# Reordering VectorE and ScalarE in the second mixer of a four-layer transformer kernel, with split gate-rank products and later splits

## What is computed

```python
def second_mixer(x):                                   # twice, L = 0 and 1
    h = rms_norm(x, norm_mix_g)
    p = h @ w_in                                       # 11 units of 256 columns, and 16 gate columns
    y_a = silu(layer_norm(conv31(a_val * sigmoid(a_gate))))     # 256 channels, 31 taps
    y_b = head_rms_norm(attention(q, k, v))                     # 4 heads
    gate_logit = p[..., 16 gate columns] @ gla_gate_w + gla_gate_b   # the gate rank
    log_a = log_sigmoid(gate_logit) / 16
    y_c = gla_chunked(q_c, k_c, v_c, log_a)            # memory: G = cumsum(log_a), state over 8 chunks
    y_c = head_rms_norm(y_c) * silu(p_r)
    return x + concatenate([y_a, y_b, y_c]) @ w_out    # 4 units
```

## Time and profile before

| | |
|---|---|
| time, median of 3 runs (lowest, highest) | 2444.72 us (2442.86, 2446.11) |
| the profiled execution's own time | 2447.14 us |
| its span, first to last instruction | 2445.2 us |
| PE busy | 2289.4 us (94%) |
| VectorE busy, ScalarE busy | 1758.5 us (72%), 1321.9 us (54%) |
| first mixer, L = 0 and 1: first product of T(0) | 19.4 and 435.7 us |
| second mixer, L = 0 and 1: transposes of the normed x | 1729.0 and 2087.8 us |
| end of the second mixer, L = 1: transposes for the feed-forward | 2237.4 us |

### The profile page before, as it was taken

One profiled execution on the slowest core, in us unless ns is written; L12 is line 12 of the kernel. 1 busy time (PEld: TensorE's weight loads), 2 busy tenths in 40 slices (PEclk: granted clock), 3 DMA queues, 4 the chain that ended last, 5 costly groups with the idle time before them and its releaser, 6 DMA issues.

```text
span 2445.2 us, 42024 instructions
## 1 busy us (share of the span) xinstructions
PE 2289.4 (94%) x16293; PEld 2136.1 (87%) x16293; DVE 1758.5 (72%) x1877; ACT 1321.9 (54%) x1254; POOL 185.5 (8%) x178
## 2 busy tenths in 40 slices
PE   7998998999699999999999999998788999798998
PEld 7898997899689999999999999998687998687997
DVE  4455555457478888888888888888676777666777
ACT  4543443554166767676767766766334444434443
POOL 1000000100000000000000000000580000660000
PEclk9999999999699999999999999999898999999999
DMA  9344655534379999999999999999323555323551
GB/s 299 104 139 142 203 187 175 153 105 145 98 272 343 347 336 352 332 353 345 341 349 335 350 333 351 334 350 332 111 88 111 173 198 176 119 95 104 191 176 63
DMA packets 423456, 556.71 MB, mean 228 GB/s; under 512 B 9746, under 2 KB 377092, under 8 KB 423344
## 3 DMA queue, kind: packets, MB, share of 16 engines
q1 hardware_dynamic: 419232, 544.85, 65.9%
q0 software_dynamic: 4112, 10.38, 1.4%
HBM read 554.13 MB, written 1.06 MB: 227 GB/s over the span
## 4 chain that ended last, share of the span: by engine, by line
issue 46%; PE 41%; DVE 5%; DVEq 3%; ACT 3%; DMA 1%; ACTq 0%; SPq 0%; POOL 0%; POOLq 0%
PE ps L616 12%; PE ps L617 12%; PE ps L618 12%; ACT w_hi L1305 2%; DVE w_lo L1691 1%; DVEq L2165 1%; PE ps L658 1%; PE ps L1187 1%; DVE cvT L2164 1%; PE ps L1132 1%; DVEq L1791 1%; PE ps L1167 1%; PE ps L807 0%; DMA raw<-in_w_in 0%; DVE x L1790 0%
## 5 line engine op out<-in xcount | busy, mean ns | idle before, releaser
L1691 DVE TENSOR_TENSOR w_lo<-raw,w_hi 128x2048 fp32r<-128x2048 f32 x519 | 1180.4, 2284 | 382.0 <-ACT w_hi L1305 380.4
L1305 ACT ACTIVATE w_hi<-raw 128x2048 fp32r<-128x2048 f32 x519 | 986.8, 1908 | 237.1 <-PE ps L618 223.3
L616 PE MATMUL ps<-w_hi,xg_hi 128*128 128x256 f32 x1792 | 515.6, 288 | 9.9 <-DVE xg_lo L2073 7.0
L616 PE MATMUL ps<-xT_hi,w_hi 128*128 128x256 f32 x1696 | 491.1, 290 | 17.4 <-DVE xT_lo L1706 8.4
L618 PE MATMUL ps<-w_hi,xg_lo 128*128 128x256 f32 x1792 | 504.6, 282 | 0.0
L617 PE MATMUL ps<-w_lo,xg_hi 128*128 128x256 f32 x1792 | 504.0, 281 | 0.0
L617 PE MATMUL ps<-xT_lo,w_hi 128*128 128x256 f32 x1696 | 485.8, 286 | 0.0
L618 PE MATMUL ps<-xT_hi,w_lo 128*128 128x256 f32 x1696 | 485.4, 286 | 0.0
L616 PEld LDWEIGHTS ps<-w_hi,xg_hi 128*128 128x128 f32 x1792 | 339.4, 189 | 17.4 <-issue 11.1
L616 PEld LDWEIGHTS ps<-xT_hi,w_hi 128*128 128x128 f32 x1696 | 331.9, 196 | 24.2 <-DVE xT_lo L1706 9.2
L617 PEld LDWEIGHTS ps<-w_lo,xg_hi 128*128 128x128 f32 x1792 | 339.5, 189 | 4.0
(11 more groups left out here) (444 smaller groups left out, 2809.9 us busy)
## 6 DMA issues: line engine op xcount, KB each, us to landing
raw<-in_exp_w SPq DMA_DIRECT2D x336, 1024.0 KB, 5.5
raw<-in_ffn_w_up SPq DMA_DIRECT2D x44, 1024.0 KB, 5.1
raw<-in_w_in SPq DMA_DIRECT2D x42, 1024.0 KB, 6.0
raw<-in_ffn_w SPq DMA_DIRECT2D x33, 1024.0 KB, 5.1
raw<-in_ffn_w_down SPq DMA_DIRECT2D x22, 1024.0 KB, 5.4
raw<-in_w_gate SPq DMA_DIRECT2D x16, 1024.0 KB, 5.4
raw<-in_w_out SPq DMA_DIRECT2D x8, 1024.0 KB, 4.9
raw<-in_w_o SPq DMA_DIRECT2D x6, 1024.0 KB, 5.6
```

The source lines that it names most:

```text
L616: pe.matmul(out, lhs[0], rhs[0], start=first, stop=False)
L1305: act.activation(w_hi[:, u.const % SPL, 0:width], raw[:, u.const % RAW, 0:width], ACT.Copy)\
L1691: dve.tensor_tensor(w_lo[:, u.const % SPL, 0:width], raw[:, u.const % RAW, 0:width], w_hi[:, u.const % SPL, 0:width].bitcast(F32), ALU.sub ...
```

## The change

Six things are altered, and nothing in what is computed but the rounding of the gate rank.

1. **Gate rank in split products.** VectorE splits `w16` into `w16_hi` and `w16_lo` once it has landed (`w16_split`), and PE's `gate_rank` makes 8 x 3 float32r matmuls for the float32 ones.
2. **The memory chain ahead of the taps.** VectorE's 13 taps, before in groups of 3, 2, 1, 3, 2 and 2 between the steps of the chain, come in groups of 4, 2, 3 and 4: four ahead of the gate logits, none from there until `atT` is masked. `ahead(3)` to `ahead(7)` each stand later in the chain, on VectorE and (`ahead(3)`) on ScalarE.
3. **PE:** head 0 of `gla_out` goes ahead of the attention scores, so PE waits for `state_ready` in front of both; the wait for `vb` moves from the first transposes to the first values.
4. **The end of the second mixer:** `gated(0)` ahead of `ahead(10)` on VectorE; the first `yM_lo` ahead of the attention's norm; on ScalarE `yM_hi` ahead of that norm's root, and `ahead(13)` ahead of the SiLU.
5. **Second splits behind the norm sums.** Of the two splits ahead of `sums_to_x` (and at the kernel's start, and at the experts' end) VectorE's second goes behind `x_parts`. ScalarE's halves stay.
6. **The z gate's sigmoid later.** `out(8)` and `out(9)` are plain copies, `out(8)` right after `am_ready`; one Sigmoid over all of `zg` follows the first pair of attention transposes (`zg_ready`).

Cut to its core:

```diff
@@ PE, gate_rank
-                    for i, part in enumerate((xT_hi, xT_lo)):
-                        for k in range(KC):
-                            m = pe.matmul(ps[0:16, 6, 0:S], w16[:, k, :], part[:, k, :].bitcast(F32),
-                                          start=i == 0 and k == 0, stop=i == 1 and k == KC - 1)
+                    pe.wait_ge(S_.w16_split, L + 1)
+                    pe.sem_inc(S_.pe_passed, 1)
+                    for k in range(KC):
+                        m = product(ps[0:16, 6, 0:S], [v[:, k, :] for v in (w16_hi, w16_lo)],
+                                    [v[:, k, :] for v in (xT_hi, xT_lo)], k == 0, k == KC - 1)
@@ PE, mixer2
                 pe.wait_ge(S_.state_ready, L + 1)
+                gla_out((0,))
                 pe.wait_ge(S_.proj2_out, L * 11 + 8)
                 scores(0, (2, 3))
                 scores(1, (4, 7))
-                gla_out()
+                gla_out((1, 2, 3))
                 tok(8)
...
-                pe.wait_ge(S_.proj2_out, L * 11 + 9)
                 pe.wait_ge(S_.expd2, L + 1)
                 next_pair(0)
-                tok(9, lambda: next_pair(1))
+
+                def first_values():
+                    pe.wait_ge(S_.proj2_out, L * 11 + 9)
+                    next_pair(1)
+
+                tok(9, first_values)
@@ ScalarE, mixer1
                 act.activation(stat[:, 24:32], ps[:, 2, 8:16], ACT.Exp, scale=-1.0).then_inc(S_.am_ready, 1)
+                out(8, zg[:, :, 0:256], bank(0, TT, 256))
                 act.drain()
...
                 split(u + 11)
-                out(8, zg[:, :, 0:256], bank(0, TT, 256), ACT.Sigmoid)
                 split(u + 12)
-                out(9, zg[:, :, 256:512], bank(1, TT, 256), ACT.Sigmoid)
+                out(9, zg[:, :, 256:512], bank(1, TT, 256))
+                act.drain()
...
                 pT_pair(0)
+                act.activation(zg[:], zg[:], ACT.Sigmoid).then_inc(S_.zg_ready, 1)
                 pT_pair(1)
@@ ScalarE, mixer2
                 act.activation(egT[:], egT[:], ACT.Ln, bias=1.0).then_inc(S_.gln_ready, 1)
+                ahead(3)
...
-                square_root(S_.sqrt2_in, S_.sqrt2_out, L * 5 + 3, stat[:, 112:120])
                 act.wait_ge(S_.yc_psum, L * 2 + 1)
                 high(yM_hi[:, 0:2, :], 3, 70)
+                square_root(S_.sqrt2_in, S_.sqrt2_out, L * 5 + 3, stat[:, 112:120])
...
+                ahead(13)
                 act.wait_ge(S_.cnorm_ready, L + 1)
...
-                ahead(13)
                 ahead(14)
@@ VectorE, mixer1 and mixer2
                 x_parts(L * 12, 4)
+                split(u + 1)
                 split(u + 2)
...
+                split(u + 1)
                 ahead(0)
                 ahead(1)
+                dve.wait_ge(S_.p2_loaded, L * 192 + 192)
+                dve.tensor_copy(w16_hi[:], w16[:])
+                dve.drain()
+                dve.tensor_tensor(w16_lo[:], w16[:], w16_hi[:].bitcast(F32), ALU.subtract).then_inc(S_.w16_split, 1)
...
                 ahead(13)
-                ahead(14)
                 sums_to_x(u + 14, L * 6 + 3, None, half_square, OUT2_BANKS)
...
                 x_parts(L * 8 + 28, 0)
+                ahead(14)
@@ VectorE, main
-                    split_next(Count(LAYER1_UNITS))
+                    split(Count(LAYER1_UNITS))
                     sums_to_x(Count(LAYER1_UNITS - 1), 0, ALPHA, half_stats)
...
-                    split_next(at + STEP * DENSE_STEPS)
+                    split(at + STEP * DENSE_STEPS)
```

More of the change, by code:

```diff
@@ L348, in build @@
                     kdz = sb("kdz", [P, TT * 2, 2, P], scope=s)
+                    w16_hi = sb("w16_hi", [P, KC, 16], F32R, scope=s)
+                    w16_lo = sb("w16_lo", [P, KC, 16], F32R, scope=s)
                 sb0 = sb("sb0", [P, HB, P], scope=m2)
@@ L1177, in scores, with gla_out @@
                     m.then_inc(S_.scores2, 1)
-                def gla_out():
-                    for h in range(GH):
+                def gla_out(heads):
+                    for h in heads:
                         rows = slice(64 * (h % 2), 64 * (h % 2) + 64)
@@ L1188, in gla_out @@
                                               start=False, stop=j == 3)
-                    m.then_inc(S_.o_psum, 1)
+                    if h == GH - 1:
+                        m.then_inc(S_.o_psum, 1)
                 def gated_T(pair):
@@ L1370, in mixer1, with out @@
             def mixer1(L, u):
-                def out(n, dst, src, func=ACT.Copy):
+                def out(n, dst, src):
                     used(u + n)
-                    act.activation(dst, src, func).then_inc(S_.proj1_out, 1)
+                    act.activation(dst, src, ACT.Copy).then_inc(S_.proj1_out, 1)
                 x_parts(L * 8, 4)
@@ L1692, in split @@
                                   w_hi[:, u.const % SPL, 0:width].bitcast(F32), ALU.subtract).then_inc(S_.lo_ready, 1)
-            def split_next(u):
-                for n in range(AHEAD):
-                    split(u + n)
             def used(u):
@@ L2198, in mixer2 @@
                 ahead(2)
-                convolve(3)
+                convolve(4)
                 dve.wait_ge(S_.glog_psum, L + 1)
@@ L2216, in mixer2 @@
                 dve.tensor_copy(gam, ends[:, :, :, GCH - 1:GCH].rearrange("p c n o -> p c (n o)")).then_inc(S_.cum_ready, 1)
-                ahead(4)
-                convolve(1)
+                ahead(3)
                 dve.wait_ge(S_.gexp_ready, L * 2 + 1)
@@ L2229, in mixer2 @@
                                       ALU.mult)
-                dve.tensor_tensor(laT[:], kcT[:], laT[:], ALU.mult)
+                dve.wait_ge(S_.gexp_ready, L * 2 + 2)
+                dve.tensor_tensor(cumT[:], kcT[:], cumT[:], ALU.mult)
                 dve.drain()
[L2232 to L2237, removed]
+                dve.tensor_tensor(qcT[:], qcT[:], egT[:], ALU.mult).then_inc(S_.qkg_ready, 1)
+                ahead(4)
                 dve.wait_ge(S_.at_psum, L + 1)
@@ L2242, in mixer2 @@
                 m.then_inc(S_.at_ready, 1)
+                ahead(5)
                 convolve(2)
+                ahead(6)
+                convolve(3)
                 ahead(7)
@@ L2286, in mixer2 @@
                 dve.tensor_tensor(cvT[:], cvT[:], conv_part[:], ALU.add).then_inc(S_.conv_ready, 1)
-                ahead(10)
                 def gated(pair):
@@ L2297, in mixer2 @@
                 gated(0)
+                ahead(10)
                 dve.wait_ge(S_.pv2, L * HB + HB)
@@ L2311, in mixer2 @@
                 m.then_inc(S_.cent_ready, 1)
+                low(yM_lo[:, 0:2, :], 3, 70, yM_hi[:, 0:2, :], 1)
                 dve.wait_ge(S_.sqrt2_out, L * 5 + 3)
@@ L2320, in mixer2 @@
                 m.then_inc(S_.yb_ready, 1)
-                low(yM_lo[:, 0:2, :], 3, 70, yM_hi[:, 0:2, :], 1)
                 gated(1)
@@ L2382, in _ @@
             dve.memset(stat[:, 4:5], 0.0).then_inc(S_.xn_ready, 2)
-            for n in range(AHEAD):
-                split(Count(n))
+            split(Count(0))
             with dve.Fori(0, 2) as L:
```

7 lines of the change are left out of this document (2 added, 5 removed).

## The result

The changed kernel takes 2417.4 us (median, 2415.0 to 2425.1), the kernel before 2445.4 beside it: a ratio of 0.9892, 95% interval 0.9879 to 0.9906. A second series of executions of the same changed kernel gave 2412.8 us and 0.9871 (0.9856 to 0.9886). The forecast was 2414, and both medians lie within 4 us of it. But the sum came out right with wrong terms in it, which is what the rest is about. Beside the runs that follow, the kernel before took 2445.4 to 2446.3 us, so the medians of different series can be compared to about 1 us.

The account below looks back on a forecast made before the run. PE, busy 94%, was taken as the bound, with waits on VectorE's chain and half clock behind them. Gains of 21.9 + 4.0 + 4.7 = 30.6 us from 2447.1 gave 2416.5, shifted to a median of 2414; range 2406 to 2426.

Parts of the forecast that it names:

- Gate rank, 3.0 us for 7.0: Second mixer: 24 float32r matmuls replace the float32 ones, so T(2) starts 4.0 us earlier.
- Rival 1: Gate rank gains nothing, still 7.0 us in split products; 4.0 us later per pass, 2422; chance 0.07.
- The pause ahead of tok(5): Second mixer: PE newly waits 4.2 us for the late split of u+5; half clock behind it taken as 0.75.
- 4.5 and 2.1 us for `cumT` and `atT`: Second mixer, memory chain: PE's waits for these two go, gaining 4.5 and 2.1 us.
- rival 4: Second mixer: pauses ahead of tok(5) and behind T(7) keep PE at half clock, slower than before, 2485.5; chance 0.02.
- 5.85: Second mixer: running gain in us per pass once the wait for `atT` is gone, ahead of the recurrence.
- `state_ready`, "PE waits about 1.5 us": At the recurrence: VectorE needs 21.0 us, PE's work 19.5, so a new wait of about 1.5 us.
- a clock at 0.50 for more than 4 us at a stretch: Granted PE clock: one of the listed signs that would make the prediction wrong.
- `vb`, `oc`, `yM_lo`: Second mixer's smaller waits: 0.7 and 0.8 us go, `yM_lo` falls from 2.1 to 0.8 with no low clock.
- Rival 2: The transfer of `w16` lands 3 us later, PE waits 3 more in both passes, 2420; chance 0.10.
- rival 3: VectorE becomes the bound at the recurrence, taps costing 2.1 us for 1.7 beside GpSimd, 2421; chance 0.10.
- Ends and first mixers: Late splits gain 2.2 us at second mixer and convolution ends, 2.5 at the dense end; late sigmoid 2.0 per first mixer.

Follow-up runs that it names:

- the taps alone: VectorE's five convolution taps ahead of the recurrence moved behind it, against the changed kernel; 2403.8 us, ratio to the kernel before 0.9827.
- the split alone: Both parts of the split of u+5 put back early, between gate logits and Ln, against the changed kernel; 2411.4 us, ratio 0.9853.
- the kernel of 2396.2: Changed kernel with five taps behind the recurrence, u+5's split early, GpSimd's taps 16 for 18, u+11's split behind cvT's sum; 2396.2 us.

## Why the prediction was right, and where it wasn't

- **Gate rank, 3.0 us for 7.0: right.** T(2) begins 18.0 us into the pass for 22.5, and the run of the rank alone bears it out. Rival 1 is out.
- **The pause ahead of tok(5), "4.2 us": there, but smaller.** 3.3 us in L = 1, 2.0 and another 0.35 behind tok(5) in L = 0; VectorE's taps ahead of the logits took 6.0 and 4.6 us for the 6.7 taken. The half clock in tok(5) came in L = 1 (48 matmuls in 7.5 us for 5.95, so the full 1.5) and not in L = 0. The Trainium skill, "TensorE: Matmul & The Clock Gate", section "HAM oscillation — how this bites in real kernels", describes a kernel in which each wait for data, of some 3 to 5 us, is followed by a stretch at half rate. The trace agrees for the 3.3 and for the waits of 3.5 and 5.3 at the recurrence. The 2.0 is shorter than the page's waits and had no low clock behind it, but in the kernel before the waits of 2.1 us did have one.
- **The clock behind the old pauses: left out of the sum.** I wrote down 4.5 and 2.1 us for `cumT` and `atT`, and nothing for what came behind them. This is the view of windows, kernel before, from `state_steps` into T(7):

```profile
2150.00:2152.00 2.00, 1.07 (x12) 1.00 0.56 84
2152.00:2160.00 8.00, 8.00 (x60) 0.57 0.54 198
2160.00:2166.00 6.00, 5.31 (x49) 1.00 0.18 60
```

  That is 8 us at 0.57, so "Before, the clock was back after 3 us each time" (rival 4) was a misreading. `state_steps` took 6.3 us there and takes 4.5 in the changed kernel, T(7) 7.3 and 6.0, the memory's scores 2.2 and 1.3. Together that is 4.7 us in L = 1 and 4.4 in L = 0. The eight passes that have the waits for `cumT` and `atT` all show a low clock in `state_steps` or T(7); of the sixteen without a wait ahead of `state_steps`, four do. At T(7)'s end the changed kernel is 11.3 us ahead in L = 1 and 13.4 in L = 0, where I had 5.85.
- **`state_ready`, "PE waits about 1.5 us": the step that failed.** It measured 3.5 and 5.3. VectorE's side was well priced (21 us, and 21.5 from `atT` to the end in L = 1); it was PE's "19.5 us" that was wrong: 16.3 in the changed kernel. I had taken PE's times from rows at half clock, and a change that takes the pause away takes that half clock away too. Behind the wait came what I had priced only in rival 4: `gla_out` and scores take 15.7 to 16.4 us in six of the eight passes for 12.7, and 21.4 in the other two, where tok(8) is 1.9 longer too: 3.0 to 3.7 us, or 10.6. At the end of `gla_out` the gain is 3.4 us in L = 1 and 1.8 or 6.7 in L = 0, where I had 5.05. Rival 4 named the right mechanism; even the long stretch is two thirds of the 15.3 us a pass from which it makes the kernel slower. The prediction had named "a clock at 0.50 for more than 4 us at a stretch" as a sign that it was wrong, and by that sign this part was wrong.
- **`vb`, `oc`, `yM_lo`:** none, none and 0.9 us are left, for none, none and 0.8; no low clock behind it. Right.
- **`w16`:** no wait, for 0.6. Its load took 4.6 us from issue to landing in the changed kernel, and 5.9 before. Rival 2 is out.
- **VectorE as the bound (rival 3):** it is the bound at the recurrence, but not through slower taps: these took 8.6 us in L = 1 and 6.3 in L = 0, for 8.4.
- **Ends and first mixers:** 2.6, 3.0 and 3.6 us of pause less at the ends of the second mixer, of the convolution and of the dense feed-forward, for 2.2, 2.2 and 2.5; behind a shorter pause there is less half clock as well, which the prediction has nowhere: over the 6 us behind the second mixer's end the clock was 0.60 and 0.62 before and 0.72 after, which is 0.6 to 0.7 us of PE's time. 3.0 and 0.7 are the 3.7 of L = 0 in the table. Of the 2.0 of L = 1, 0.6 are from the sooner clock; the other 1.5 are a stretch of half clock that the kernel before has behind PE's wait of 2.0 us at 2262 (0.61 and 0.54 in two windows of 2 us), and neither profile of the change. In the first mixers the wait of 2.5 us for `zg` became one of 0.2 to 0.5 for `pT`, 2.0 to 2.3 us each for 2.0; the stretches gave 2.2 and 1.9.

So the sum of 30.6 was right in good part by luck. In the second mixer two omissions of opposite sign met: the old half clock, 4.4 to 4.7 us a pass, and the recurrence, where the longer wait and the half clock behind it cost 7.2 us more than I had in L = 1, and 12.6 or 5.8 in L = 0. In the first profile the two second mixers gave 16.3 us for the 21.9 of the sum, and all the rest 13.4 for 8.7. The parts add up roughly: 9.4, 4.0 and 10.9 us are 24.3 of the 28.0 to 32.6 that the whole change gives. What remains, 4 to 8 us, is put down to the new order on VectorE and the second mixer's end, the larger part of the diff; no run has these alone. It is small because VectorE's queue gives much of it back at the recurrence, as the run with five taps moved shows.

## What to carry to other kernels

A duration read behind a pause holds the clock of that pause: before it goes into a sum, look at its window, and take the price from a row at the clock that the engine will have after the change. When a chain is moved ahead of filler work, the filler needs a place where no one waits: here five taps between three splits cost 9 to 14 us because they stood ahead of the recurrence; behind it no wait for them showed. And when PE comes earlier by several us, list each engine's last delivery on that stretch anew: the one that ends next was GpSimd, which no wait of the kernel before named.

## What the runs showed of the hardware

- The granted clock can fall while PE is busy throughout: 8 us at 0.57 in `state_steps` and T(7), 9 to 18 us behind the last wait. Of the sixteen passes in which PE didn't wait right ahead of `state_steps` (the changed kernel twice and all its variants), four show a drop there, worth 1.5 to 3 us: L = 1 with the taps alone, L = 0 with the split alone, and both of the kernel of 2396.2. `state_steps` is 56 matmuls of 32x128. Why it falls in one pass and not in another is open.
- How long the clock stays low differs between two executions of the same program at the same wait (24 us and 10 at 3.5 us), with PE busy all through the 24. The spread of this kernel's times goes with it: of its eight executions the fastest (2409.3 us) has the highest mean clock, 0.971, and the slowest (2425.1) the lowest, 0.961. With the taps moved, and the wait gone, four executions lie within 1.5 us.
- Half a tap (one instruction, 128x256) on VectorE is slower beside GpSimd, and by how much varies. The timeline of VectorE, changed kernel, twice beside GpSimd's taps (L = 0 and L = 1) and once behind them (in L = 1 they end at 2158.9):

```profile
1771.31 2.11 DVE L2169 SCALAR_TENSOR_TENSOR cvT<-avT,cols,cvT 128x256 f32<-128x256 f32 x4
...
2128.02 5.29 DVE L2169 SCALAR_TENSOR_TENSOR cvT<-avT,cols,cvT 128x256 f32<-128x256 f32 x6
...
2159.53 3.74 DVE L2169 SCALAR_TENSOR_TENSOR cvT<-avT,cols,cvT 128x256 f32<-128x256 f32 x8
```

  0.53 and 0.88 us an instruction beside GpSimd, 0.47 behind it. So a tap that moves to where GpSimd has ended is cheaper too; in the run of the taps alone, L = 0, GpSimd was still at work, and the moved taps took 0.65 an instruction.
